# Feed-forward stages that start from unscaled pieces of x, apply 1/rms when results leave PSUM, and round their inner activations on ScalarE

## What is computed

```
def _layer_norm(x, g, b):  mu, var = mean, variance over features;  (x - mu) * rsqrt(var + 1e-5) * g + b
def _rms_norm(x, g):       x * rsqrt(mean(x * x) + 1e-6) * g
def _swiglu(x, w1, w3, w2): (silu(x @ w1) * (x @ w3)) @ w2        # w1, w3: 1024 x 2816, w2: 2816 x 1024

# first block, layer l (a = 4 ** 0.25)
x = ln1(a * x + 0.5 * swiglu(x, ffn1))
x = ln2(a * x + token_mixing(x))
x = ln3(a * x + cross_attention(x, mem))
x = ln4(a * x + 0.5 * swiglu(x, ffn2))
# second block, layer l
x = x + 0.5 * swiglu(rms(x, g0), ...)
x = x + mixer(rms(x))                  # gated linear attention + RG-LRU (l = 0), HGRN2 (l = 1)
x = x + 0.5 * swiglu(rms(x, g1), ...)
x = x + sigmoid(rms(x) @ gate) * (p @ proj)
# rms at the end
```

## Time and profile before

| | |
|---|---|
| median of 3 runs | 2988.86 us (2987.72 to 2989.83) |
| profiled execution | 2990.64 us, of which the span of instructions is 2988.8 us |
| PE busy | 2774.5 us, 93% of the span |
| POOL busy | 2198.4 us, 74% |
| DVE busy | 1391.4 us, 47% |
| ACT busy | 1381.2 us, 46% |
| HBM read | 448.72 MB, 150 GB/s over the span |
| PE clock granted over the span | 0.968 of full speed |

### The profile page before, as it was taken

The page is one execution under the profiler, slowest core; times in us unless marked ns, Lnnn a source line. Parts: engine busy times, 40 slices in busy tenths (PEclk is TensorE's granted clock), DMA queues, the critical chain, the costliest instruction groups (busy, mean ns, idle before and its releaser), DMA issues.

```text
span 2988.8 us, 59411 instructions
## 1 busy us (share of the span) xinstructions
PE 2774.5 (93%) x21913; PEld 2667.2 (89%) x21920; DVE 1391.4 (47%) x2270; ACT 1381.2 (46%) x2025; POOL 2198.4 (74%) x1680
## 2 busy tenths in 40 slices
PE   8999999979999989999969999997899899998997
PEld 8989998868999989898968989996899899888997
DVE  3344435544344344435544344357434633644335
ACT  4444455444444444456434444445444644555444
POOL 8976666746978967575647968976699599766994
PEclk9999999989999999899989999999899999999999
DMA  6544343424544544343424544543455355443552
GB/s 237 183 148 154 133 141 126 157 85 140 182 164 155 182 151 151 118 155 120 156 92 141 182 142 156 182 147 113 142 186 182 114 191 182 147 133 129 189 181 76
DMA packets 122979, 451.83 MB, mean 151 GB/s; under 512 B 13650, under 2 KB 13650, under 8 KB 122196
## 3 DMA queue, kind: packets, MB, share of 16 engines
q1 hardware_dynamic: 121104, 441.43, 44.2%
q10 hardware_dynamic: 1732, 8.39, 0.8%
HBM read 448.72 MB, written 1.05 MB: 150 GB/s over the span
## 4 chain that ended last, share of the span: by engine, by line
POOL 59%; issue 29%; PE 9%; DVE 1%; POOLq 1%; ACT 1%; DVEq 0%; ACTq 0%
POOL wl L364 30%; POOL wl L363 29%; PE R L398 2%; PE R L401 2%; PE R L402 2%; PE R L523 1%; PE Y L398 1%; PE Y L402 1%; PE Y L401 1%; POOLq L369 0%; PE R L428 0%; PE R L431 0%; PE R L434 0%; DVE W L1754 0%; DVE XL L1747 0%
## 5 line engine op out<-in xcount | busy, mean ns | idle before, releaser
L363 POOL TENSOR_TENSOR wl<-raw,wh 128x512 fp32r<-128x512 f32 x836 | 1106.7, 1324 | 768.7 <-ACT wh L1049 754.8
L1049 ACT ACTIVATE wh<-raw 128x1024 fp32r<-128x1024 f32 x836 | 883.0, 1058 | 818.4 <-PE R L398 493.3
L398 PE MATMUL R<-XH,wh 128*128 128x256 f32 x4216 | 1209.8, 287 | 14.1 <-DVE XL L2006 6.4
L401 PE MATMUL R<-XL,wh 128*128 128x256 f32 x4216 | 1198.8, 284 | 0.0
L402 PE MATMUL R<-XH,wl 128*128 128x256 f32 x4216 | 1198.5, 284 | 0.0
L364 POOL TENSOR_TENSOR wl<-raw,wh 128x512 fp32r<-128x512 f32 x836 | 1139.9, 1363 | 0.0
L398 PEld LDWEIGHTS R<-XH,wh 128*128 128x128 f32 x4216 | 815.1, 193 | 21.2 <-POOL wl L364 11.4
L401 PEld LDWEIGHTS R<-XL,wh 128*128 128x128 f32 x4216 | 815.3, 193 | 1.3 <-issue 1.0
L402 PEld LDWEIGHTS R<-XH,wl 128*128 128x128 f32 x4216 | 814.8, 193 | 0.0
L398 PE MATMUL Y<-BH,wh 128*128 128x256 f32 x1408 | 399.3, 284 | 0.9
L401 PE MATMUL Y<-BL,wh 128*128 128x256 f32 x1408 | 398.4, 283 | 0.0
(11 more groups left out here) (362 smaller groups left out, 3122.7 us busy)
## 6 DMA issues: line engine op xcount, KB each, us to landing
raw<-in_stream SPq DMA_DIRECT2D x836, 512.0 KB, 3.3
G<-in_wcmp ACTq DMA_DIRECT2D x2, 2048.0 KB, 7.5
G<-in_mem ACTq DMA_DIRECT2D x2, 1024.0 KB, 6.1
TB<-in_table SPq DMA_DIRECT2D x1, 1312.0 KB, 12.3
X<-in_x SPq DMA_DIRECT2D x2, 512.0 KB, 5.7
out_dram<-X ACTq DMA_DIRECT2D x4, 256.0 KB, 2.2
WS<-in_mix_w ACTq DMA_DIRECT2D x2, 256.0 KB
G<-in_p ACTq DMA_DIRECT2D x2, 256.0 KB, 2.6
```

Source lines behind the costliest of these rows:

```text
L363: pool.tensor_tensor(wl[:, s, 0:512], raw[:, r, 0:512], wh[:, s, 0:512].bitcast(F32), ALU.subtract)
L398: i = pe.matmul(o, wh[w], hi, start=start, stop=False, skip_group_check=True)
L401: pe.matmul(o, wh[w], lo, start=False, stop=False, skip_group_check=True)
L1049: act.activation(wh[:, n % SPLIT, :], raw[:, n % RAW, :], ACT.Copy).then_inc(hi_done, 1)
```

## The change

Names are those of the new kernel where they differ.

1. **Pieces without the root.** In front of the seven normed stages `pieces` and `piece_of_x` split `gain * x` (LayerNorm: `gain * (x - mean)`) directly; the root isn't needed for that. ACT rounds a chunk (`piece`: Identity with the gain as scale) and squares two chunks at a time. DVE makes `XL` in one instruction. Behind the mixers this is done while the mixer's output blocks still run (`last_splits`, and `add_chunks` with a gain).
2. **The sum of squares by one matmul.** DVE adds the 8 squared chunks by three additions of 1024, 512 and 256 elements (`late_root`). PE does the one ones-matmul between the two up blocks of hidden chunk 1. Its result shares a bank with the mean (LayerNorm) or claims one (RMS), and the second up block needs that bank back.
3. **1/rms at eviction.** DVE makes S3 = root and S4 = root / 4, and every w1 chunk is multiplied by S3, every w3 chunk by S4, as it leaves PSUM (`hidden_rms`, `hidden_ln`).
4. **LayerNorm's bias as two more columns.** The bias is two extra columns (256 and 257) of the pieces, so all up matmuls of these three stages are 258 columns wide, and the product of bias and weights comes out in column 256. DVE copies it to `BB`; ACT adds it to the w1 part, DVE to the w3 part. `X` itself is scaled inside the stage (`scaled`, two DVE instructions for each of 8 chunks, one chunk in each of the turns j = 2 to 9).
5. **Inner activations rounded by ScalarE.** The rounding to `BH` goes from DVE to ACT (`rounded`), in all eight stages. ACT's order in a turn becomes: tanh, round a block, round the activation, round two blocks. In the first up phase three blocks are rounded instead of two.
6. `XH` and `XL` become views of tiles with 258 columns.

```diff
+                if kind != "first":
+                    trips -= 1
+                    for j in range(4):
+                        dense(hi, lo, width=width)
+                        if j == 0:
+                            need(sq_summed)
+                            pe.matmul(sums[:, T:2 * T], ONES, W8[:, 0, :], start=True, stop=True,
+                                      skip_group_check=True).then_inc(chunk_ready, 1)
+                        dense(hi, lo, width=width)
+                        down(j)
...
+            def piece(c, gain):
+
+                from_dve()
+                give_dve(act.activation(XH[:, c, :], X[:, c, :], ACT.Identity, scale=gain(c)))
+                if c % 2 == 1:
+                    act.activation(flat(W8[:, c - 1:c + 1, :]), flat(X[:, c - 1:c + 1, :]), ACT.Square).then_inc(x_squared, 1)
...
+            def late_root(eps):
+
+                m = t.n["chunk"]
+                act.wait_ge(chunk_ready, m + 4)
+                skip(1)
+                step(act.activation(S2[:, 0:T], R[:, m % RING, T:2 * T], ACT.Ln, scale=1.0 / D, bias=EPS[:, eps:eps + 1]))
+                give_dve(act.activation(S3[:, 0:T], S2[:, 0:T], ACT.Exp, scale=-0.5))
+                act.preload_act_table_set("exp_and_others")
...
                 def pair(j):
+                    gate(j)
                     split_next()
-                    hidden(j)
+                    rounded(j)
                     split_next()
...
+            def hidden_rms(j):
+                e, h, a, v = EB[:, j % 2, :], HID[:, j % 2, :], M[:, 2 + j % 2, :], HID[:, 2 + j % 2, :]
+                m, o = chunk()
+                give_act(tt_(a, o[:, 0:T], S3[:, 0:T], ALU.mult))
+                from_act()
+                take(stt(e, e, 1.0, o[:, 0:T], ALU.add, ALU.mult), m)
+                m, o = chunk()
+                take(tt_(v, o[:, 0:T], S4[:, 0:T], ALU.mult), m)
+                give_act(tt_(h, e, v, ALU.mult))
+                split_hidden(j)
...
+            def hidden_ln(j):
+                e, h, a, v = EB[:, j % 2, :], HID[:, j % 2, :], M[:, 2 + j % 2, :], HID[:, 2 + j % 2, :]
+                b1, b3 = BB[:, j % 2, 0:1], BB[:, j % 2, 1:2]
+                m, o = chunk()
+                step(tt_(a, o[:, 0:T], S3[:, 0:T], ALU.mult))
+                take(dve.tensor_copy(b1, o[:, T:T + 1]), m)
+                dve.sem_inc(dve_act, 1)
+                t.up(dve_act)
+                from_act()
+                step(stt(e, e, 1.0, a, ALU.add, ALU.mult))
+                m, o = chunk()
+                tt_(v, o[:, 0:T], S4[:, 0:T], ALU.mult)
+                take(ts_(b3, o[:, T:T + 1], 0.25, None, ALU.mult), m)
+                give_act(stt(h, v, b3, e, ALU.add, ALU.mult))
+                split_hidden(j)
...
+                def scaled(c):
+
+                    step(stt(X[:, c, :], X[:, c, :], gain(c), S3[:, 0:T], ALU.mult, ALU.mult))
+                    step(ts_(X[:, c, :], X[:, c, :], bias(c), None, ALU.add))
...
+            def late_root(eps):
+
+                need(x_squared, 4)
+                step(tt_(flat(W8[:, 0:4, :]), flat(W8[:, 0:4, :]), flat(W8[:, 4:8, :]), ALU.add))
+                step(tt_(flat(W8[:, 0:2, :]), flat(W8[:, 0:2, :]), flat(W8[:, 2:4, :]), ALU.add))
+                give(tt_(W8[:, 0, :], W8[:, 0, :], W8[:, 1, :], ALU.add), sq_summed)
```

More of the change, by code:

```diff
@@ L487, in piece_ready, with means, ffn @@
                     need(outs_split)
-            def ffn(ready):
+            def means(wait):
+                o = claim()
+                for c in range(DC):
+                    wait(c)
+                    i = pe.matmul(o[:, 0:T], ONES, X[:, c, :], start=c == 0, stop=c == DC - 1, skip_group_check=True)
+                i.then_inc(mean_ready, 1)
+                return o
+            def ffn(kind, sums=None):
+                hi, lo, width = (XHB, XLB, T + 2) if kind == "ln" else (XH, XL, T)
                 for b in range(4):
@@ new lines, in pieces, with last_splits @@
+            def pieces(gain, bias=None):
+                act.preload_act_table_set("natural_log_exp_and_others")
+                if bias is not None:
+                    give_dve(act.activation(XHB[:, :, T:T + 2], bias.unsqueeze(2).to_broadcast([P, DC, 2]), ACT.Copy))
+                for c in range(DC):
+                    piece(c, gain)
+            def last_splits(gain):
+                for c in range(DC - 1):
+                    split_next()
+                    if c == 0:
+                        act.preload_act_table_set("natural_log_exp_and_others")
+                    for p in {1: (0,), 2: (1, 2), 3: (3,), 4: (4,), 5: (5,), 6: (6, 7)}.get(c, ()):
+                        piece(p, gain)
+                skip(DC)
@@ new lines, in ffn @@
+            def ffn(kind, late=None, gain=None, bias=None):
+                hidden = {"first": hidden_first, "rms": hidden_rms, "ln": hidden_ln}[kind]
+                def scaled(c):
+                    step(stt(X[:, c, :], X[:, c, :], gain(c), S3[:, 0:T], ALU.mult, ALU.mult))
+                    step(ts_(X[:, c, :], X[:, c, :], bias(c), None, ALU.add))
+                hidden(0)
+                if kind == "ln":
+                    for j in range(1, FC - 1):
+                        hidden(j)
+                        if 2 <= j < 2 + DC:
+                            scaled(j - 2)
+                else:
+                    per = {"chunk": 8, dve_pe: 4, act_dve: 8, dve_act: 4 if kind == "first" else 8,
+                           **{("round", b): 2 for b in range(RING)}}
+                    with dve.Fori(0, (FC - 2) // 4) as it:
+                        t.enter(it, per)
+                        for j in range(4):
+                            hidden(j + 1)
+                        t.leave((FC - 2) // 4)
```

230 lines of the change are left out of this document (141 added, 89 removed).

## The result

The changed kernel takes 2966.19 us (median of 4 runs, 2961.87 to 2967.48) against 2989.15 us before (4 runs beside it, 2987.72 to 2989.83): a ratio of 0.9921, with an interval of 0.9905 to 0.9937. The profiled execution took 2967.48 us.

The account below looks back on a forecast made before the run. Feed-forward stages were taken to run at PE's pace, one matmul every 0.12 us. Boundary gains of 20.3 less 2.7 (width), 3.9 (stage ends) and 9.1 (slow clock) gave 4.6 us: 2988.86 to 2984.3 us, range 2972 to 3002.

Parts of the forecast that it names:

- matmuls on 258-wide tiles keep another distance: Sign of being wrong: up matmuls of LayerNorm stages not 0.121 us apart as forecast; given no chance.
- LayerNorm, three: Three LayerNorm boundaries, first subtraction to down(0): 21.9 us, 3.75 us earlier each, 11.3 us gained.
- behind mixers, two: RMS boundaries behind the two mixers: down(0) 3.25 us earlier each, 6.5 us gained.
- gated embedding: RMS boundary behind the gated embedding: down(0) at 2388.4 against 2390.52, 2.1 us gained.
- ln4 of layer 1: RMS boundary behind ln4 of layer 1: down(0) at 1809.9 against 1810.34, 0.4 us gained.
- (a) width: Up matmuls of three LayerNorm stages: two more columns at 0.43 ns each cost 2.7 us.
- (b) stage ends: Before down(21): PE idle 0.9 us, 0.6 more in seven stages, first stage gains 0.3; 3.9 us lost together.
- (c) slow clock behind down(0): After idle time before down(0), PE runs at half clock: one stretch in each of seven stages, 9.1 us lost.
- (d) inside the stages: Turns inside the stages: DVE and ACT work stays under PE's pace, taken as 0 loss.
- The clock at no cost: Faster rival: the granted clock drops inside idle time, so (c) slow clock behind down(0) vanishes; 2975.2 us, chance 0.20.
- DVE late in LayerNorm stages: Slower rival: in turns 2 to 9 DVE exceeds 8.67 us; 3011 us, or 2998 at half of that; chance 0.20.
- The table load on the path: No-gain rival: ACT's load between Exp and first tanh, standing 1.4 us longer, delays down(0); 2990.1 us, chance 0.12.

Follow-up runs that it names:

- e4_at_256: Changed kernel with 320 columns of room per row of the two wide tiles and a narrower zeros tile, streamed rows on multiples of 256 bytes; 2992.4 us, ratio 1.0005.
- e2_warm: Changed kernel with matmuls of zeros in PE's idle time before the second up block and down(0) of seven stages; 2958.48 us, ratio 0.9881.
- e2_old_tiles: Changed kernel with all tiles at their old places, XH and XL 256 wide, bias left out of the result; 2985.6 us, ratio 0.9981.
- e1_round: Kernel before with only ScalarE rounding the inner activation instead of VectorE, weight blocks in the changed kernel's order; 2987.04 us, ratio 0.9994.
- e1_pad: Kernel before with one unused tile of 128 bytes a partition in front of XH, nothing else; 2971.26 us, ratio 0.9933.
- e4_8: Kernel before with XH and XL 8 bytes, BH and BL 48 bytes past a multiple of 256 behind the weights' tiles; 2956.32 us in its profiled execution.

## Why the prediction was wrong

**The step that failed.** "No row reads a tile with rows of 258 elements; `XL` and `XH` in the mixers are taken at no cost", and ahead of it the 0.12 us of the earlier trace rows, taken for what PE needs. I priced two more columns and not where they put the other tiles. I had named it among the signs of being wrong ("matmuls on 258-wide tiles keep another distance"), but gave it no rival and no chance; and it was the tiles of 256 that took another distance, in all stages and mixers. By the distances its size is about 19 us, which with my 4.6 makes the 23 measured and a little more. From e4_at_256 to the changed kernel it is 25 us by the two ratios (1.0005 and 0.9921); what is over lies in part in the slow clock, which differs between the two profiled executions: behind the last stage the changed kernel is 4.2 us shorter, with 9.7 us at half clock where e4_at_256 has 19.8.

**The rest of the sum**, read in e4_at_256, where PE keeps the old pace; each boundary from the last matmul ahead of it to down(0):

| term | forecast | measured |
|---|---|---|
| LayerNorm, three | 11.3 | 11.5 (29.49 to 25.65 each) |
| behind mixers, two | 6.5 | 5.9 (22.07 to 19.01, 21.89 to 19.04) |
| gated embedding | 2.1 | 2.1 (25.47 to 23.33) |
| ln4 of layer 1 | 0.4 | -0.5 (38.13 to 38.58) |
| (a) width | -2.7 | -2.9 (120.83 - 119.92 ns, 3168 times) |
| (b) stage ends | -3.9 | about +0.4 |
| second matmul of down(0) | none | -0.7 (0.1 us late, seven times) |
| (c) slow clock behind down(0) | -9.1 | about -10.6, the rest of the stages' 13.8 (26 us at half clock) |
| (d) inside the stages | 0 | 0, no gap of PE in turns 2 to 9 |

The boundaries give 19.0, the eight stages last 13.8 us longer from down(0) on: 5.2 net, where the forecast had 4.6. That these are so near is partly luck: (b) was 4.3 too dear, and the boundaries, the clock, the width and the second matmul were together 3.7 too cheap. Of the terms only (b) was much off. I had added hand-overs at down(21) as if none lay beside PE's work; the row of the changed kernel, LayerNorm, has PE 0.31 us idle, as the earlier trace rows had PEld, and the distance to the matmul ahead is 0.58 us where it was 0.39:

```profile
1080.17 0.28 PE L405 MATMUL Y<-BH,wl 128*128 128x256 f32 x1
1080.75 0.39 PE L401 MATMUL Y<-BH,wh 128*128 128x256 f32 x1 [0.31 <-DVE BL L1722]
```

In the RMS stages behind the mixers the wait is gone, as in the first stage; in the other two RMS stages 0.23 us are left. The group of the low pieces in the changed kernel tells why, 857 ns each in the mean where the earlier trace rows has 1404 (in front of down(21) 0.43 to 0.89 us, forecast 1.4); they run into POOL's halves far less than I took:

```profile
L1722 DVE TENSOR_TENSOR BL<-W,BH 128x256 fp32r<-128x256 f32 x176 | 150.8, 857 | 93.9 <-ACT BH L1179 93.9
```

**What then ate the 5 us.** In e4_at_256 the parts that the change does not touch, four mixers, the embedding and the end, take 6.8 us longer than before in the two profiled executions. The largest is layer 1's first mixer with cross-attention, from the last down block to the last output block, before and then e4_at_256:

```profile
1093.05:1563.91 470.86, 428.75 (x3352) 399.21 (x3351) 226.39 (x475) 226.63 (x410) 285.40 (x219) 0.94 0.39 130
```

```profile
1088.94:1562.86 473.92, 431.50 (x3352) 401.23 (x3351) 227.66 (x475) 226.36 (x410) 285.83 (x219) 0.94 0.38 129
```

3352 matmuls in both, 3.06 us apart. Of these 2.90 come up within 1162 matmuls, between which PE hardly waits, again before and then e4_at_256:

```profile
1124.54:1257.97 133.43, 132.04 (x1162) 126.70 (x1161) 64.72 (x107) 60.30 (x96) 90.39 (x69) 0.93 0.42 138
```

```profile
1120.93:1257.26 136.33, 134.95 (x1162) 129.01 (x1161) 64.94 (x107) 60.29 (x96) 89.75 (x69) 0.91 0.40 134
```

The same work, at a mean clock of 0.91 in place of 0.93. The head of the next mixer shows it closer, 55.85 us from the end of the stage:

```profile
1989.15:2045.00 55.85, 42.36 (x247) 36.66 (x246) 40.27 (x59) 28.03 (x48) 31.07 (x24) 0.91 0.33 109
```

```profile
1990.04:2045.89 55.85, 43.45 (x241) 37.62 (x240) 40.27 (x59) 27.16 (x46) 31.72 (x25) 0.85 0.31 106
```

The idle times of PE are the same (4.56 us, then 3.9), but behind each of them the half clock lasts 6.83 us in place of 3.41, so the mean clock is 0.85 in place of 0.91 and six matmuls fewer are done. Over all the parts that the change does not touch, e4_at_256 is at half clock for 176.8 us and before for 157.3; of these PE has a matmul in work for 134.6 and 117.5, and 17 us at half speed cost about 8. How long a stretch lasts differs between executions of the same code (in the changed kernel it is 3.41 behind both of the two idle times, in e2_warm 3.41 behind the first and 6.83 behind the second), and in e2_old_tiles the same parts take only about 3 us longer than before. Ten runs of e4_at_256 spread from 2988.65 to 2993.77, so it is not one odd execution; why this program meets the longer stretches more often stays open. My term (c) priced the idle time that the change makes and took all other idle time as it was.

**The rivals.** The clock at no cost: refuted by e2_warm. DVE late in LayerNorm stages: no gap there, though DVE is busy 49.26 of 80 us. The table load on the path: it takes 1.28, the rounding starts 0.01 behind its end, at 897.62, and then ACT waits 0.60 for DVE. The Trainium skill's second figure there (ScalarE: Activation LUTs, What ACT_TABLE_LOAD costs, 1380 ns of drain) shows nowhere in this trace either.

## What to carry to other kernels

A change that widens a tile moves every tile behind it. Before a gain or loss is put down to the work that was changed, run the old kernel with an unused tile of the same size; it costs one line. In a kernel whose time is matmuls back to back, try a few places of the streamed tiles against the tiles in front of them (here 16 bytes past a multiple of 256, worth 1.6%), and count matmuls in a busy stretch at full clock rather than trust one distance. And where idle time is moved in front of matmuls that set the pace, matmuls of zeros in it can pay for themselves (here 7.7 us).

## What the runs showed of the hardware

The distance of fp32r matmuls of 256 columns, each with a new weight tile, depends on where the streamed rows begin against the tiles in front of them, weights included: 120.0 ns on multiples of 256 bytes, 116.8 ns at 16 past it, and between them it neither rises nor falls steadily (118.0 at 32, 119.9 at 64, 118.9 at 128). On a multiple of 256 nearly all distances are 120 (17,565 of 18,444 in the kernel before), though in a stage of e1_round they repeat 118, 121, 120, 124, 117, with the same mean; elsewhere they repeat in short patterns such as 113, 116, 118, 120, and the same placement can hold another pattern in another stage (e1_pad). Two columns more cost 0.91 ns on multiples of 256, 1.2 in the changed kernel, and about 3 at offset 16, more than columns alone can explain. What in the chip makes these patterns was not found.

The Trainium skill (TensorE: Matmul & The Clock Gate, Back-to-back issue gap) gives 262 cycles at 256 columns for isolated matmuls, 109 ns; no placement here came below 116.8. The Trainium skill (SBUF — State Buffer, Door 1: The DMA port swizzle) tells of lines of 16 bytes in SBUF, and that an access that crosses to a new line pays a penalty. By that, rows that begin 8 bytes off a line should be no faster than rows that begin on one; in e4_8 they stand 117.1 ns apart, against 119.9 at offset 0 and 116.8 to 117.4 at 16, so lines of 16 bytes alone do not order these numbers.
